# RMSNorm factors applied at other places of a one-core decoder step on Trainium2

## The chip, the cores and the metric

The kernel runs on one core of one Trainium2 chip. The metric is the device time of one execution in microseconds. A kernel's time is the median of several runs; the profile is of one execution of its own.

## The reference, cut to what matters

One step of a decoder trunk for 256 prompt tokens and 8 x 4 sample tokens, 288 in all, 2048 features, all f32:

```python
def rmsnorm(x, g):
    return x * rsqrt(mean(x * x, -1) + EPS) * g

x = x + mixing_block(rmsnorm(x, norm_mix))       # w_in, convolutions, gated scan, w_out
k, v = rmsnorm(mem, norm_mem) @ (w_k, w_v)       # 256 memory tokens
x = x + cross_attention(rmsnorm(x, norm_xattn), k, v)   # w_q, scores, values, w_o
x = x + hier_moe(rmsnorm(x, norm_moe))           # logits = h @ (wg, we) + bias, top-2 experts of 16
y = rmsnorm(x, norm_final)
```

RMSNorm multiplies each token by a factor of its own (1/rms) and each feature by a weight of its own (the gain). A product h @ w may take the token's factor before or after it; the gain belongs to the features that the product sums over, so it must stand before it.

## The kernel before, in words

Activations are kept transposed, features on the 128 partitions: xT, hT and mT (the memory) have 16 blocks of [128, 288] (256 for the memory). Each engine has a program of its own; they meet at semaphores.

**Projections** (`project`, L730 to L761). A weight matrix is cut into tiles of 512x512 (1 MB). w_in (first of three parts) has 16 tiles, w_mid 8, w_last 16, w_k 16, w_out 16, w_q 16, w_v 16, w_o 16. Each tile is multiplied by a seven-product scheme of Strassen's kind on 2x2 blocks. That needs sums of weight blocks, which GpSimd makes per tile in four operations (`sum_tile`, L652 to L657), and sums of activation blocks, which VectorE makes per group of four blocks in four operations (`h_sums`, L1414 to L1422). Four tiles (one column group) accumulate in PSUM; VectorE combines the seven products in place in six operations (`combine`, L1441 to L1447), and ScalarE copies the result out. PSUM has eight banks in two halves of four; units of work take the halves in turn (`start_unit` waits until the half is read out, `half_free`).

**Loads.** SyncE (SP) issues nearly all loads in program order: x, 16 small loads of norm weights, biases and states (`pack`), the memory, the gate weights, then the weight tiles into a ring whose places TensorE frees. GpSimd and TensorE wait for each tile.

**Entry.** TensorE transposes x (three chunks of tokens), the memory (two) and pack (L695). VectorE squares x; a matmul with a column of 1/2048 sums the squares (`stat`, L722), VectorE copies the partial sums, a second matmul with ones adds and spreads them (L727), ScalarE takes the root, VectorE the reciprocal (`apply_norm`, L1469) and multiplies each block by weight and factor (L1471), with `h_sums` after every fourth block. The first matmul of w_in needs the first group. The memory takes the same way.

**Mixing block.** After w_in come the gates (`gates(0)`, L778, 16 small matmuls), w_mid, gates again, w_last; GpSimd and VectorE do the scan. The key projection runs (`project_memory`, L799), its last four tiles behind `mix_stat`; VectorE normalises the 16 blocks of the mixed output in two halves (L1643), each fourth followed by `h_sums`, and after them combines the last key columns (`combine_memory("w_k", 3)`). ScalarE evicts these at L1234, TensorE transposes the states (L836), w_out starts.

**Cross-attention and router.** After w_out VectorE adds the result to xT (`add_residual`, L1650 to L1658), ScalarE squares it, statistic, root, reciprocal, normalisation with sums, w_q. After w_o the same, into hT; then the router's 16 matmuls, a copy, three small products that give the logits by token, three times 16 transposes of h for the experts (h_tok, evicted by ScalarE), and the choice of experts on VectorE (from L1754). The experts' weights stream through 12 slots.

## Time and profile before

| | us |
|---|---|
| runs | 1607.52, 1609.87, 1611.09 |
| median | 1609.87 |
| the profiled execution: its own time | 1609.71 |
| its span in the profile | 1608.0 |
| TensorE (matmul) busy | 1483.1 (92%) |
| GpSimd busy | 657.1 (41%) |
| VectorE busy | 583.6 (36%) |
| ScalarE busy | 175.2 (11%) |
| read from memory | 369.3 MB, 234 GB/s over the span |

Own time and span differ by 1.7 us around the profile's first and last instruction. On the chain of work that ended last, TensorE holds 85% of the span, VectorE 11%, ScalarE 2%. TensorE's two clock levels are 1.2 and 2.4 GHz; the profile gives the granted clock as a share of the higher one, 0.96 on the mean. "Idle before" names how long an engine stood before an operation and what released it.

### The profile page before, as it was taken

The page shows a single profiled execution, that of the slowest core. Times are in us where ns is not written, and L with a number is a line of the kernel's source. Part 1 is how long each engine was busy: PE and PEld are TensorE (multiplying, and loading weights), DVE is VectorE, ACT ScalarE, POOL GpSimd, SP SyncE. Part 2 cuts the span into 40 slices and gives each one's busy share as a digit, 9 for nine tenths or more (in the row PEclk, how much of TensorE's full clock was granted, in tenths as well). Part 3 has the DMA queues.
Part 4 walks back from the last instruction along what each step waited for, and adds up shares of the span by engine and source line. Part 5 has one row for each costly group of instructions (what it writes and reads, how often), then busy time and mean ns, then how long its engine had stood idle before and what let it go on. Part 6 is the DMA issues. An engine that isn't in the chain of part 4 may idle for free.

```text
span 1608.0 us, 24420 instructions
## 1 busy us (share of the span) xinstructions
PE 1483.1 (92%) x9906; PEld 1154.6 (72%) x9906; DVE 583.6 (36%) x1042; ACT 175.2 (11%) x281; POOL 657.1 (41%) x498
## 2 busy tenths in 40 slices
PE   5789999999959979999999899869999999999996
PEld 3789999998859969988777699754554454545534
DVE  3927668749561241112111621241212112212204
ACT  3000221000000000012222100121000000000002
POOL 4557697879947737753444557200000000000000
PEclk9889999999979989999999999979999999999998
DMA  7234444445534434463888434808999999999971
GB/s 236 79 118 145 130 158 131 157 157 186 174 104 147 153 105 150 146 259 128 325 327 330 146 132 157 340 1 354 397 422 399 396 423 397 379 423 397 400 311 59
DMA packets 106097, 376.99 MB, mean 234 GB/s; under 512 B 12405, under 2 KB 12405, under 8 KB 76274
## 3 DMA queue, kind: packets, MB, share of 16 engines
q1 hardware_dynamic: 103762, 371.68, 61.3%
q10 hardware_dynamic: 2272, 4.42, 0.8%
q8 instruction: 45, 0.74, 0.2%
q14 instruction: 18, 0.15, 0.0%
HBM read 369.30 MB, written 6.77 MB: 234 GB/s over the span
## 4 chain that ended last, share of the span: by engine, by line
PE 85%; DVE 11%; ACT 2%; issue 1%; DMA 1%; DVEq 0%; ACTq 0%; SPq 0%
PE ps L752 36%; PE ps L1048 14%; PE ps L799 11%; PE ps L1096 7%; PE ps L1110 4%; PE ps L1026 4%; PE ps L856 2%; DVE hT L1471 2%; DVE hT L1643 1%; PE ps L1065 1%; PE ps L874 1%; PE ps L864 1%; DVE hT L1420 1%; DMA A<-in_x_sample 1%; PE ps L695 1%
## 5 line engine op out<-in xcount | busy, mean ns | idle before, releaser
L752 PE MATMUL ps<-hT,tiles 128*128 128x144 f32 x2816 | 470.7, 291 | 49.3 <-ACT kv_stage L1234 16.8
L752 PEld LDWEIGHTS ps<-hT,tiles 128*128 128x128 f32 x2816 | 401.6, 194 | 52.8 <-issue 23.8
L652 POOL TENSOR_TENSOR tiles<-tiles 128x512 f32<-128x512 f32 x88 | 123.4, 1402 | 228.8 <-DMA tiles<-in_w_in 89.8
L1048 PE MATMUL ps<-tiles,A 128*64 128x512 f32 x576 | 171.2, 601 | 1.3 <-DVE A L1876 1.3
L752 PE MATMUL ps<-tiles 128*128 128x144 f32 x960 | 172.1, 289 | 0.0
L1441 DVE COPY pair_sums<-ps 128x144 f32<-128x144 f32 x44 | 13.5, 308 | 354.6 <-PE ps L752 354.6
L752 PEld LDWEIGHTS ps<-tiles 128*128 128x128 f32 x960 | 141.3, 193 | 0.0
L752 PE MATMUL ps<-A,tiles 128*128 128x144 f32 x768 | 138.2, 289 | 0.0
L799 PE MATMUL ps<-tiles,mT 128*128 128x256 f32 x512 | 133.3, 383 | 4.1 <-ACT kv_stage L1234 4.1
L655 POOL TENSOR_TENSOR tiles<-tiles 128x512 f32<-128x512 f32 x88 | 122.8, 1396 | 0.0
L657 POOL TENSOR_TENSOR tiles<-tiles 128x512 f32<-128x512 f32 x88 | 118.3, 1344 | 6.9
L654 POOL TENSOR_TENSOR tiles<-tiles 128x512 f32<-128x512 f32 x88 | 118.0, 1341 | 6.9
L1048 PEld LDWEIGHTS ps<-tiles,A 128*64 128x64 f32 x576 | 52.9, 138 | 88.3 <-issue 86.2
L752 PEld LDWEIGHTS ps<-A,tiles 128*128 128x128 f32 x768 | 113.5, 193 | 0.0
L1096 PE MATMUL ps<-tiles,mT 128*64 128x512 f32 x448 | 113.3, 597 | 0.0
L1048 PE MATMUL ps<-A 128*64 128x512 f32 x384 | 112.9, 593 | 0.0
L799 PEld LDWEIGHTS ps<-tiles,mT 128*128 128x128 f32 x512 | 94.0, 191 | 23.2 <-ACT kv_stage L1234 6.8
L799 PE MATMUL ps<-tiles,A 128*128 128x256 f32 x384 | 103.8, 379 | 0.0
L642 POOL TENSOR_TENSOR tiles<-tiles 128x512 f32<-128x512 f32 x32 | 45.6, 1425 | 101.5 <-DMA tiles<-in_xa_w_v 91.7
L1887 DVE TENSOR_TENSOR mT<-mT,ps 64x512 f32<-64x512 f32 x16 | 11.0, 689 | 201.9 <-ACT mT L1348 201.9
L799 PEld LDWEIGHTS ps<-tiles,A 128*128 128x128 f32 x384 | 73.0, 190 | 9.9
L1096 PEld LDWEIGHTS ps<-tiles,mT 128*64 128x64 f32 x448 | 36.7, 138 | 54.1 <-issue 54.1
(287 smaller groups left out, 1741.6 us busy)
## 6 DMA issues: line engine op xcount, KB each, us to landing
tiles<-in_expert_w_down SPq DMA_DIRECT2D x56, 1024.0 KB, 10.0
tiles<-in_w_in SPq DMA_DIRECT2D x40, 1024.0 KB, 5.1
tiles<-in_expert_w_gate SPq DMA_DIRECT2D x40, 1024.0 KB, 11.3
A<-in_expert_w_up SPq DMA_DIRECT2D x32, 1024.0 KB, 9.4
tiles<-in_expert_w_up SPq DMA_DIRECT2D x32, 1024.0 KB, 12.6
...
```

The costliest lines, as they stand in the source:

```text
L642: step.tick(tt(t1, b12, b11, ALU.subtract))
L652: step.tick(tt(s1, a21, a22, ALU.add))
L654: tt(a21, a11, a21, ALU.subtract)
L655: step.tick(tt(s2, s1, a11, ALU.subtract))
L657: tt(s4, a12, s2, ALU.subtract).then_inc(weights_summed, 1)
L752: return mm(one(u + mp, x, TH), w[:, kp, mp, :], rhs, start=(first and g == 0 and kp == 0), stop=(g == 3 and kp == 1), skip_group_check=True)
L799: return mm(one(u, x, TW // 2), own, w[:, kp, :], start=(first and g == 0 and kp == 0), stop=(g == 3 and kp == 1), skip_group_check=True)
L856: m = nc.tensor.transpose(attention_bank(i % 2)[:, b * P:(b + 1) * P], cache_tile(tile)[:, (4 * (i % 4) + b) * P:(4 * (i % 4) + b + 1) * P ...
L1026: mm(ps[:, b // 4, b % 4 * P:(b % 4 + 1) * P], h_tok[:, c, b * P:(b + 1) * P], pick[:, c, :], start=(b % 4 == 0 and c == 0), stop=False, s ...
L1048: m = mm(ps[C * n:C * n + C, BRANCH_BANK, :], xe[:, b, C * s:C * s + C], moe_tile(t + 2 * g + n).rearrange("p (k n) -> p k n", k=KT)[:, k, :],
L1096: m = mm(ps[C * s:C * s + C, 4 + b, :], actT[:, s, k, :], moe_tile(16 + 2 * k + s)[:, b * TW:(b + 1) * TW], start=(k == 0), stop=(k == KT ...
L1110: m = mm(ps[:, scatter_bank(q) + b, 0:T], y_pair[:, j * P:(j + 1) * P], spread[:, :], start=True, stop=True)
```

## The change

At five places the factors of RMSNorm are put elsewhere.

1. **Entry.** x's tokens lie on the partitions when they are loaded. ScalarE squares each chunk with a running sum, takes the root; VectorE takes the reciprocal and scales the identity by it (`diag`). The product of a chunk of x with this diagonal is the transposed chunk times its factors (`turn_scaled`); the weights are applied when it is evicted, half by VectorE, half by ScalarE (`scaled_out`). The statistics on TensorE go. x is still transposed as it is, too: chunk 0 before, chunks 1 and 2 after. The load of x has three semaphores; pack's loads go to ScalarE's queue; the first four tiles of w_in are issued right after x, memory and gate weights after them.
2. **Memory.** Its two diagonal products come between w_in and the gates.
3. **w_k.** `combine_memory("w_k", 3)` comes after blocks 0 to 7 of the mixed output instead of after all 16.
4. **w_out to w_q.** `add_residual` also multiplies by the weights alone and makes the sums; w_q runs on that. The statistic's matmuls come after w_q's fourth tile, the product with ones after its fifth, in a spare bank; the queries are multiplied by the factors at their eviction by VectorE (group 0 afterwards). Arrays change places in memory.
5. **Router.** hT gets the weights alone, too. Per group of four blocks come the router's matmuls, the statistic's, and between them the first transposes for the experts. The logits and the statistic are brought to the tokens together; ScalarE takes the root (`token_root`), VectorE multiplies the logits by the factor, ScalarE multiplies h_tok at its eviction.

The diff, cut to its core; the pieces are SyncE's loads, TensorE's program (entry, memory, w_q, router), ScalarE's (squares, eviction), and VectorE's (entry, mixed output, `add_residual`, queries, logits):

```diff
-sp.dma_start(x_nat[:, 0:2, :], a["x_prompt"][0].rearrange("(c p) d -> p c d", p=P)).then_inc(x_loaded, 16)
-sp.dma_start(x_nat[0:NB * ST, 2, :], a["x_sample"].rearrange("b t d -> (b t) d")).then_inc(x_loaded, 16)
...
+for c in range(2):
+    sp.dma_start(x_nat[:, c, :], a["x_prompt"][0, c * P:(c + 1) * P, :]).then_inc(x_loaded[c], 16)
+sp.dma_start(x_nat[0:NB * ST, 2, :], a["x_sample"].rearrange("b t d -> (b t) d")).then_inc(x_loaded[2], 16)
+def load_mem_and_gates():
+    sp.dma_start(mem_nat[:, :, :], a["mem_prompt"][0].rearrange("(c p) d -> p c d", p=P)).then_inc(mem_loaded, 16)
...
+if name == "w_in" and j == RAW - 1:
+    load_mem_and_gates()
...
+def turn_scaled(u, src, scale, rows):
+    start_unit(pe, u)
+    for b in range(DB):
+        m = mm(bank(u, b // 4)[:, b % 4 * P:b % 4 * P + rows], src[:, b * P:(b + 1) * P], scale,
+               start=True, stop=True)
+    m.then_inc(unit_done, 1)
+turn_x(UNIT["x"], 0)
 for c in range(3):
     rows = P if c < 2 else NB * ST
-    turn(UNIT["x"] + c, lambda b: x_nat[0:rows, c, b * P:(b + 1) * P], rows)
-pe.wait_ge(mem_loaded, 16)
+    pe.wait_ge(diag_ready, c + 1)
+    turn_scaled(UNIT["h"] + c, x_nat[0:rows, c, :], diag[0:rows, c, 0:rows], rows)
 for c in range(2):
-    turn(UNIT["mem"] + c, lambda b: mem_nat[:, c, b * P:(b + 1) * P], P)
-pe.wait_ge(pack_loaded, 16 * 16)
-turn(UNIT["pack"], lambda b: pack[0:NROWS, b * P:(b + 1) * P], NROWS, GB)
+    turn_x(UNIT["x_rest"] + c, c + 1)
...
-stat("x_stat", [(mean_d, hT, range(DB), T)], squares_ready, (1, 1, 0), groups=False)
-stat("mem_stat", [(mean_d, mem_sq, range(DB), NM)], mem_sq_ready, (2, 2, 1), groups=False)
...
+project("w_in", 2, hT, h_sums_in)
+pe.wait_ge(mem_loaded, 16)
+for c in range(2):
+    pe.wait_ge(mem_diag_ready, 1)
+    turn_scaled(UNIT["mem"] + c, mem_nat[:, c, :], diag[:, c, :], P)
 pe.wait_ge(wbd_loaded, 16 * 4)
 pe.wait_ge(xc_ready, 1)
 gates(0)
...
+project("w_out", 2, hT, h_sums_out)
+spare_bank = lambda mp: ps[:, 4 * ((UNIT["w_q"] + mp) % 2) + 3, 0:T]
+for j in range(16):
+    project_tile("w_q", j, h_res, h_sums_q)
+    if j == 3:
+        for k in range(DB):
+            if k % 4 == 0:
+                pe.wait_ge(squares_ready, 1 + k // 4 + 1)
+            c = 32 * (k % 4)
+            m = mm(spare_bank(0)[c:c + 32, :], mean_d[:, :], sq_res[:, k, :], start=(k < 4), stop=(k >= DB - 4))
+        m.then_inc(unit_done, 1)
+    if j == 4:
+        pe.wait_ge(partial_ready, 2)
+        mm(spare_bank(1), ones[:, :], rstd[:, 0, :], start=True, stop=True).then_inc(unit_done, 1)
...
+def route(g):
+    pe.wait_ge(h_ready, 4 * HREADY["moe"] + g + 1)
+    for k in range(4 * g, 4 * g + 4):
+        c = 32 * (k % 4)
+        mm(bank(u, 0)[c:c + 32, 0:T], wr[:, k, :], hT[:, k, :], start=(k < 4), stop=(k >= DB - 4))
+    pe.wait_ge(squares_ready, 5 + g + 1)
+    for k in range(4 * g, 4 * g + 4):
+        c = 32 * (k % 4)
+        m = mm(bank(u, 1)[c:c + 32, 0:T], mean_d[:, :], sq_res[:, k, :], start=(k < 4), stop=(k >= DB - 4))
+    return m
...
+for g in range(3):
+    route(g)
+start_unit(pe, UNIT["h_tok"])
+turn_tokens(0, range(12))
+route(3).then_inc(unit_done, 1)
+turn_tokens(0, range(12, 16)).then_inc(unit_done, 1)
+pe.wait_ge(logits_in, 1)
+pe.wait_ge(stat_out, 1)
 for c in range(3):
     own = rstd[:, 0, c * P:(c + 1) * P] if c < 2 else rstd[:, 1, 0:P]
-    m = mm(bank(u, c)[:, 0:NG + NE], own, same_logit[:, :], start=True, stop=True)
+    mm(bank(u, 2)[:, 32 * c:32 * c + NG + NE], own, same_logit[:, :], start=True, stop=True)
+    m = mm(bank(u, 2)[:, 32 * c + 20:32 * c + 21], stat_sum[:, c * P:(c + 1) * P], ones[:, 0:1], start=True, stop=True)
...
+    fn(spare[0:rows, :], x_nat[0:rows, c, :], ACT.Square, accum_out=mean_sq[0:rows, c:c + 1]).then_inc(squared, 1)
+    act.wait_ge(squared, c + 1)
+    fn(token_rstd[0:rows, c:c + 1], mean_sq[0:rows, c:c + 1], ACT.Sqrt, scale=1.0 / D,
+       bias=consts[0:rows, 0:1]).then_inc(mean_root, 1)
+def scaled_out(name, u, dst, rows):
+    for b in range(GB):
+        r = ROWS[name] + 1
+        m = fn(dst[:, GB + b, 0:rows], bank(u, 2 + b // 4)[:, b % 4 * P:b % 4 * P + rows], ACT.Copy,
+               scale=vec[:, b, r:r + 1])
+    m.then_inc(half_free[u % 2], 1)
...
+def make_diag(c):
+    rows = P if c < 2 else NB * ST
+    dve.wait_ge(mean_root, c + 1)
+    then(v.reciprocal(token_rstd[0:rows, c:c + 1], token_rstd[0:rows, c:c + 1]))
+    ts(diag[0:rows, c, 0:rows], ident[0:rows, 0:rows], token_rstd[0:rows, c:c + 1], None, ALU.mult
+       ).then_inc(diag_ready, 1)
+def scaled_out(name, u, dst, rows):
+    gains = vec[:, :, ROWS[name]].rearrange("p (b k) -> p b k", k=4).unsqueeze(3).broadcast_to([P, 2, 4, rows])
+    tt(dst[:, 0:GB, 0:rows].rearrange("p (b k) n -> p b k n", k=4), from_banks(u, rows)[:, 0:2], gains, ALU.mult
+       ).then_inc(half_free[u % 2], 1)
+make_diag(0)
+u = UNIT["x"]
+after_event(dve, EVENT["x"])
+v.tensor_copy(quads(xT[:, :, 0:P]), from_banks(u)).then_inc(half_free[u % 2], 2)
+make_diag(1)
+read_out(dve, UNIT["pack"])
 for c in range(3):
-    read_out(dve, UNIT["x"] + c)
-tt(hT[:, :, :], xT[:, :, :], xT[:, :, :], ALU.mult).then_inc(squares_ready, 1)
-read_out(dve, UNIT["pack"])
-lam = vec[:, :, ROWS["rg_lambda"]]
-stt(out=small[:, 0, :], in0=lam, scalar=-1.0, in1=lam, op0=ALU.mult, op1=ALU.max).then_inc(lam_in, 1)
+    after_event(dve, EVENT["h"] + c)
+    scaled_out("norm_mix", UNIT["h"] + c, hT[:, :, c * P:T], P if c < 2 else NB * ST)
+    if c == 0:
+        make_diag(2)
...
+for g in range(4):
+    h_sums(hT, h_sums_in, g)
+u = UNIT["x_rest"] + 1
+after_event(dve, EVENT["x_rest"] + 1)
+v.tensor_copy(quads(xT[:, :, 2 * P:T]), from_banks(u, NB * ST)).then_inc(half_free[u % 2], 2)
...
-            h_sums(h_sums_out, 2 * n + b // 4)
-combine_memory("w_k", 3)
-def add_residual(name):
+            h_sums(hT, h_sums_out, 2 * n + b // 4)
+    if n == 0:
+        combine_memory("w_k", 3)
...
+        for mp in range(2):
+            read_out(dve, group_unit(name, g, mp))
+        for b in range(4 * g, 4 * g + 4):
+            m = ts(dst[:, b, :], xT[:, b, :], gain(norm, b), None, ALU.mult)
+        if sums is not None:
+            then(m)
+            h_sums(dst, sums, g)
+        else:
+            m.then_inc(h_ready, 1)
+add_residual("w_out", "norm_xattn", h_res, h_sums_q)
...
+def evict_queries(g, scaled):
+    for mp in range(2):
+        u = group_unit("w_q", g, mp)
+        combine_pair("w_q", g, mp)
+        dve.wait_ge(combined, 2 * (GROUP["w_q"] + g) + mp + 1)
+        q = qT[:, 4 * g + 2 * mp:4 * g + 2 * mp + 2, :]
+        if scaled:
+            tt(q, half(u, T, 2), rstd[:, 0, :].unsqueeze(1).broadcast_to([P, 2, T]), ALU.mult
+               ).then_inc(half_free[u % 2], 2)
+        else:
+            v.tensor_copy(q, half(u, T, 2)).then_inc(half_free[u % 2], 2)
+evict_queries(0, False)
+after_event(dve, EVENT["xattn_stat"])
+v.tensor_copy(rstd[:, 0, :], ps[:, 4 * (UNIT["w_q"] % 2) + 3, 0:T]).then_inc(partial_ready, 1)
+dve.wait_ge(xattn_root, 1)
+then(v.reciprocal(rstd[:, 0, :], rstd[:, 0, :]))
+for mp in range(2):
+    read_out(dve, group_unit("w_q", 0, mp))
+tt(qT[:, 0:4, :], qT[:, 0:4, :], rstd[:, 0, :].unsqueeze(1).broadcast_to([P, 4, T]), ALU.mult
+   ).then_inc(first_queries_ready, 1)
+for g in range(1, 4):
+    evict_queries(g, True)
...
+dve.wait_ge(token_root, 1)
+then(v.reciprocal(h_rstd[:, 0:3], h_rstd[:, 0:3]))
 for c in range(3):
-    m = tt(lg[:, c, :], bank(u, c)[:, 0:NG + NE], rbias[:, :], ALU.add)
+    m = stt(out=lg[:, c, :], in0=bank(u, 2)[:, 32 * c:32 * c + NG + NE], scalar=h_rstd[:, c:c + 1], in1=rbias[:, :],
+            op0=ALU.mult, op1=ALU.add)
```

**TensorE at the entry**, before: transposes (L695: x in three rows, memory within the third, pack last), statistics, then w_in at the branch of its loop.

```order
L695 MATMUL ps<-ident,A 128x128 x32
L695 MATMUL ps<-ident,A 128x32 x16
L695 MATMUL ps<-ident,A 128x128 x32
L695 MATMUL ps<-ident,A 128x71 x8
L722 MATMUL ps<-hT,mean_d 32x288 x16
L727 MATMUL ps<-rstd,ones 128x288
L722 MATMUL ps<-A,mean_d 32x256 x16
L727 MATMUL ps<-rstd,ones 128x256
L736 UNCONDITIONAL_BRANCH
```

Now (L690 transposes, L708 products with the diagonal, `rstd` being where the diagonal lies):

```order
L690 MATMUL ps<-ident,A 128x71 x8
L690 MATMUL ps<-ident,A 128x128 x16
L708 MATMUL ps<-rstd,A 128x128 x32
L708 MATMUL ps<-rstd,A 128x32 x16
L690 MATMUL ps<-ident,A 128x128 x16
L690 MATMUL ps<-ident,A 128x32 x16
L778 UNCONDITIONAL_BRANCH
```

Pack is first; the memory and both statistics are gone from here; the branch is w_in's loop.

**VectorE at the end of the mixing block**, before: the third and fourth group of four normalised blocks (L1643) with their sums, then the combine of the last key columns (`tiles<-ps`).

```order
L1420 TENSOR_TENSOR hT<-hT 128x2x144
L1421 TENSOR_TENSOR A<-hT,A 128x288
L1422 TENSOR_TENSOR A<-hT,A 128x288
L1643 SCALAR_TENSOR_TENSOR hT<-hT,vec,rstd 128x288 x4
L1419 TENSOR_TENSOR A<-hT 128x288
L1420 TENSOR_TENSOR hT<-hT 128x2x144
L1421 TENSOR_TENSOR A<-hT,A 128x288
L1422 TENSOR_TENSOR A<-hT,A 128x288
L1441 COPY tiles<-ps 128x256
L1442 TENSOR_TENSOR tiles<-ps,tiles 128x256
L1443 TENSOR_TENSOR ps<-ps,tiles 128x256
L1445 TENSOR_TENSOR tiles<-ps,tiles 128x512
L1446 TENSOR_TENSOR ps<-ps,tiles 128x512
```

Now the same, from the second group on (L1745 is the old L1643, L1514 to L1517 the sums, L1536 to L1542 the combine):

```order
L1745 SCALAR_TENSOR_TENSOR hT<-hT,vec,rstd 128x288 x4
L1514 TENSOR_TENSOR A<-hT 128x288
L1515 TENSOR_TENSOR hT<-hT 128x2x144
L1516 TENSOR_TENSOR A<-hT,A 128x288
L1517 TENSOR_TENSOR A<-hT,A 128x288
L1536 COPY tiles<-ps 128x256
L1537 TENSOR_TENSOR tiles<-ps,tiles 128x256
L1538 TENSOR_TENSOR ps<-ps,tiles 128x256
L1540 TENSOR_TENSOR tiles<-ps,tiles 128x512
L1541 TENSOR_TENSOR ps<-ps,tiles 128x512
L1542 TENSOR_TENSOR ps<-ps,tiles 128x256
L1745 SCALAR_TENSOR_TENSOR hT<-hT,vec,rstd 128x288 x4
```

The combine stands behind the second group's sums instead of the fourth's; the third and fourth group follow it.

**TensorE between w_out and w_q**, before: the end of w_out's loop, the statistic (L722, L727), the loop of w_q.

```order
L736 COMPARE_AND_BRANCH
L722 MATMUL ps<-A,mean_d 32x288 x16
L727 MATMUL ps<-rstd,ones 128x288
L736 UNCONDITIONAL_BRANCH
L736 ISA
L313 ISA
L752 MATMUL ps<-hT,tiles 128x144 x2
```

Now (L756 is the old L752, L862 and L866 the statistic, L881 the values stage behind w_q):

```order
L778 COMPARE_AND_BRANCH
L756 MATMUL ps<-A,tiles 128x144 x112
L862 MATMUL ps<-A,mean_d 32x288 x16
L756 MATMUL ps<-A,tiles 128x144 x28
L866 MATMUL ps<-rstd,ones 128x288
L756 MATMUL ps<-A,tiles 128x144 x308
L881 MATMUL ps<-ident,tiles 128x128 x8
```

w_q begins at once (112 matmuls are its first four tiles), the statistic and the product with ones lie inside it.

## Rows read from the trace of the kernel before

**Rows 1.** Stretches by engine: stretch, us, busy PE, PEld, DVE, ACT, POOL, clock, DMA, GB/s
```profile
24.00:25.00 1.00, 1.00 (x11) 1.00 (x10) 1.00 (x1) 0.24 (x1) 0.88 (x1) 0.94 1.04 401
50.00:55.00 5.00, 5.00 (x24) 5.00 (x23) 4.83 (x12) 0.00 (x0) 0.00 (x0) 0.52 0.00 0
147.00:174.00 27.00, 27.00 (x218) 26.78 (x217) 19.93 (x34) 1.16 (x2) 20.11 (x16) 1.00 0.46 150
456.00:457.00 1.00, 0.00 (x0) 0.00 (x0) 1.00 (x1) 0.00 (x0) 0.76 (x1) 1.00 0.24 90
582.00:595.00 13.00, 3.60 (x34) 1.25 (x34) 8.58 (x18) 1.66 (x2) 5.05 (x4) 0.70 0.23 81
1087.00:1567.00 480.00, 477.62 (x2613) 233.32 (x2611) 86.99 (x144) 30.55 (x55) 0.00 (x0) 0.99 0.95 393
```
**Rows 2.** Timeline, TensorE at the entry: start us, us, engine, operation [idle before <-releaser]
```profile
11.57 7.57 PE L695 MATMUL ps<-ident,A 128*128 128x128 f32 x48 [11.57 <-DMA A<-in_x_sample]
21.43 4.99 PE L695 MATMUL ps<-ident,A 128*128 128x128 f32 x32 [2.29 <-ACT xT L1153]
48.95 1.32 PE L752 MATMUL ps<-hT,tiles 128*128 128x144 f32 x4 [10.55 <-DVE tiles L1422]
```
**Rows 3.** Timeline, TensorE at the fifth tile of w_in
```profile
87.02 1.33 PE L752 MATMUL ps<-hT,tiles 128*128 128x144 f32 x4 [7.50 <-ACT A L1185]
```
**Rows 4.** Timeline, ScalarE, GpSimd and VectorE at the entry
```profile
30.37 1.91 ACT L1159 ACTIVATE A<-mT 128x2048 f32<-128x2048 f32 x1
...
24.12 3.34 POOL L652 TENSOR_TENSOR tiles<-tiles 128x512 f32<-128x512 f32 x1 [19.96 <-DMA tiles<-in_w_in]
46.17 1.36 POOL L657 TENSOR_TENSOR tiles<-tiles 128x512 f32<-128x512 f32 x1
64.25 4.41 POOL L652 TENSOR_TENSOR tiles<-tiles 128x512 f32<-128x512 f32 x1 [16.72 <-DMA tiles<-in_w_in]
...
45.01 1.40 DVE L1419 TENSOR_TENSOR tiles<-hT 128x288 f32<-128x288 f32 x1
47.77 0.45 DVE L1421 TENSOR_TENSOR tiles<-hT,tiles 128x288 f32<-128x288 f32 x1
```
**Rows 5.** DMA issues: count, KB each, median us from issue to landing
```profile
A<-in_x_prompt SPq DMA_DIRECT2D x1, 2048.0 KB, 8.3
out_p_mem_k<-kv_stage ACTq DMA_DIRECT2D x4, 512.0 KB, 2.9
out_p_mem_v<-kv_stage ACTq DMA_DIRECT2D x4, 512.0 KB, 9.2
```
**Rows 6.** Timeline, TensorE at the first gates (L778) and in the experts (L1026)
```profile
175.96 2.37 PE L778 MATMUL ps<-A,kv_stage 128*128 128x312 f32 x8 [0.68 <-ACT A L1195]
179.12 0.73 PE L752 MATMUL ps<-hT,tiles 128*128 128x144 f32 x4 [0.79 <-ACT A L1203]
...
1116.88 2.94 PE L1026 MATMUL ps<-A 128*128 128x128 f32 x24
```
**Rows 7.** Timeline, key projection to w_out: TensorE, VectorE, ScalarE
```profile
451.51 1.04 PE L836 MATMUL ps<-ident,states 128*54 128x128 f32 x8
469.39 1.33 PE L752 MATMUL ps<-hT,tiles 128*128 128x144 f32 x4 [16.85 <-ACT kv_stage L1234]
...
448.06 1.41 DVE L1422 TENSOR_TENSOR A<-hT,A 128x288 f32<-128x288 f32 x1
465.38 0.42 DVE L1441 COPY tiles<-ps 128x256 f32<-128x256 f32 x1
468.33 1.01 ACT L1234 COPY kv_stage<-ps 128x1024 f32<-128x1024 f32 x1 [39.99 <-DVE ps L1447]
```
**Rows 8.** Timeline, TensorE at the start of w_q
```profile
595.25 1.32 PE L752 MATMUL ps<-hT,tiles 128*128 128x144 f32 x4 [6.51 <-DVE A L1422]
```
**Rows 9.** Timeline, VectorE: last residual addition behind w_o, first gate operation
```profile
1036.32 0.76 DVE L1658 TENSOR_TENSOR xT<-xT,ps 128x576 f32<-128x576 f32 x1
1056.37 0.17 DVE L1754 TENSOR_REDUCE mT<-mT 128x3 f32<-128x12 f32 x1
```

More of the change, by code:

```diff
@@ L227, in build @@
         place_gate, at = cut(at, 2)
+        h_rstd, at = cut(at, 4)
         silu, at = cut(at, TW)
@@ L772, in gates, with project @@
+            def project(name, pairs, h, sums):
+                with pe.Fori(0, pairs) as i:
+                    for j in range(8):
+                        project_tile(name, j, h, sums, i)
             def gates(h):
```

331 lines of the change are left out of this document (169 added, 162 removed).

## The prediction

> **What bounds the kernel now.** I read the stretches by engine first, then the engines' timelines round every place where TensorE stands. Inside a projection TensorE is never idle: 218 matmul records fill 27.00 us, 0.124 us each, and a weight tile is 56 records, so 6.9 us [rows 1]. Inside the experts it is busy 477.62 of 480 us [rows 1]. So time can only be won between the stages, and whatever TensorE starts earlier there, everything behind it ends earlier. Five places matter.
>
> At the entry the first projection matmul starts at 48.95 us, after 10.55 us of waiting for VectorE's sums [rows 2]. It then runs at the lower clock (granted 0.52 over 50 to 55, the 1.2 GHz level; 24 records in 5 us) [rows 1]; I put the end of tile 0 at 58.8 (24 records by 54.8, 32 more at 0.124). Four tiles later TensorE stands again until 87.02, 7.5 us, since VectorE first works off some forty small preparatory operations, many of them beside a working GpSimd [rows 3]; it comes back at the lower clock (four records in 1.33 us), about 5.9 us at half speed, 2.9 us lost. Between the key projection and w_out it waits 16.85 us for an eviction that ScalarE makes at 468.33, once VectorE has combined the last key columns, which stands behind all 16 normalised blocks [rows 7]. Between w_out and w_q it does 3.60 us of work in 13 us [rows 1] and starts w_q at 595.25 at the lower clock [rows 8]. Behind w_o the last residual addition ends at 1037.08, and the first gate operation starts only at 1056.37 [rows 9].
>
> **The change, part by part.** The sum is made against the profiled execution's own 1609.71 us (span 1608.0); the median of the runs, 1609.87, is practically the same.
>
> Entry. Removed ahead of the projection: three transposes of x in a row, the memory's transposes and squares, both statistics, the root with its table load, a reciprocal, 16 normalisations. Added: pack and x0 transposed, then products of x with a diagonal. The w_in loads are issued right behind x, the pack's 16 small loads on ScalarE's queue.
> - x_prompt's 2 MB landed 8.3 us after issue [rows 5]; its first half now has its own semaphore. ScalarE issues 16 loads (0.3 us each, to 5.7), loads a table, squares each chunk in about 1.9 us [rows 4]: the first two roots are there by 12, before TensorE wants them.
> - The pack is first in TensorE's order. When it lands is not shown; a load on ScalarE's queue beside few others took 2.9 us, beside a full SP queue 9.2 [rows 5]. From the last issue at 5.4 that is 8.3 or 14.6. These are a few rows, not 512 KB, so I take 9.5.
> - Pack and x0 transposes: 48 transposes took 7.57 us at the start [rows 2], so about 3.5 us for 24: 13.0. A chunk's product is 16 matmuls, 32 records, at 0.12 (24 in 2.94 us [rows 6]) or twice that at the lower clock. With the rise some 6 us after TensorE's first work: 17.8, 21.3, and 22.9 for the sample rows.
> - ScalarE evicts half a chunk by 8 small activations (2.0 us; last 24.8), so VectorE begins its 16 sum operations at 24.9. Beside a working GpSimd each takes 1.40 us, alone 0.45 [rows 4]. GpSimd starts when w_in tile 0 lands, about 13 (2.36 MB of x, then 1 MB, at some 400 GB/s), and its 16 operations, 24.12 to 47.5 before [rows 4], now last to about 34.5. So: 7 slow ones, 9 quick ones, 39.0. Only then VectorE copies out the sample rows of x, which free the half for the second half of tile 0: **late next** is this copy, 39.8. Tile 0 ends at about 44.0. Gain 58.8 - 44.0 = **14.8**. Bounds: all 16 quick and no late pack, 36; all slow with the pack at 14.6, 56.
> - VectorE's preparatory work then falls into GpSimd's pause (waiting for tile 4, as in the 16.72 us before [rows 4]) and ends near 48; its first combine is due at 61. The stall and its cold restart go: **10.4** (0 if that work took 13 us more).
>
> The memory products, 32 matmuls or 64 records, come between w_in and the gates: 64 x 0.12 = 7.7, of which the 0.8 us that TensorE waited there covers a little. Their evictions, the table load and four sigmoids follow; second gate product and the next projection started at 175.96 and 179.12 [rows 6]; I count 184.9. Cost **5.8** (4.5 to 8). The eviction of group 3 and the gates queue behind it by the same amount.
>
> Key projection to w_out. The combine moves ahead of blocks 8 to 15. TensorE ends the projection at 451.5, VectorE the second sums at 449.47 [rows 7]; combine (2.9, its time before, 465.4 to 468.3), eviction 1.0: w_out starts at 455.9 instead of 469.39, **13.5**. The third and fourth sums are done by 476 even if all their operations are slow, when tiles 2 and 3 want them at 469.6 and 476.5: just covered; late next are these. An idle stretch from 452.5 had not lowered the clock by 457 [rows 1], so half of the 2.6 us of restart, **1.3**, may go too (0 to 2.6).
>
> w_out to w_q. Squares, statistic, root, reciprocal and normalisation leave the gap; 16 products with a weight vector and 16 sum operations move beside w_out, where VectorE mostly waits for TensorE. The statistic's 32 records and the ones product stay on TensorE, 2.7 us, inside w_q. The queries' evictions move from ScalarE to VectorE, hidden by tiles of 6.9 us. Gap 13.3 (582 to 595.25) - 2.7 + 2.9 of slow restart = **13.5** (11 to 15).
>
> Behind w_o. Of 1037.1: four products with the weights 1.3, last route 1.6, transposes beside it, copy 0.8, 12 short matmuls 1.6, ScalarE's copy of h and table load (1043 to 1044.2), root 0.2, reciprocal and logits 0.6: gate operations at 1045.1 instead of 1056.37 [rows 9], **11.1**. Everything behind keeps its order, the scaled token copies cost no more than the copies. Bounds 8 and 13. The experts' first 12 tiles wait for w_o's tiles, not for the router, and are there either way.
>
> Sum: 14.8 + 10.4 - 5.8 + 13.5 + 1.3 + 13.5 + 11.1 = 58.8; 1609.71 - 58.8 = 1550.9, so **1551 us**.
>
> **A rule against the trace.** At 24 to 25 us the granted clock is already at 0.94 [rows 1], while TensorE had done nothing but transposes since 21.43 [rows 2]: here they did raise it. The Trainium skill (TensorE: Matmul & The Clock Gate, Part 4: PE-mode transpose) states that transposes do not count as work for this. By that rule the first diagonal products would start the count: all 32 records of the first chunk slow, 2 us more, a sum of 1553.
>
> **The rivals.**
> - The entry gains less: the pack's small loads come through only behind SP's queue (9.2 against 2.9 us [rows 5]), or VectorE's sums all run beside GpSimd. For it: 16 loads against 6 MB in flight. Against: they are few packets. With the pack at 14.6 everything ahead of tile 0 moves by 5, and contention may add 5: 1556 to 1561.
> - Transposes do not raise the clock: 1553. Against it speaks the rise at 24; for it, that the 48 transposes before showed no quicker pace in 6 us. The page named above states it.
> - w_out starts early but waits: the sums of blocks 8 to 15 come late at tile 2 or 3, since VectorE has them behind the combine. For it: only 0.8 us of cover at tile 3. It gives back up to 7 us: 1558.
> - The change does not free the logits or w_q: a wait on a root takes the place of the statistic's (the router's root behind ScalarE's copy and table load, say). One of the two gains gone: 1562 to 1565.
> - Slower: GpSimd becomes the bound. Its four sums per tile take about 5.4 us (1.36 each beside VectorE [rows 4]), against TensorE's 6.9. The weight products and sums now run on VectorE beside w_out and w_o, and each locks with a GpSimd operation. From 6.9 us per tile this decides; to eat the 58.8 us over the 32 tiles of w_out and w_o a tile would have to take 8.7 us, its four operations 2.2 each; the one of 3.34 us [rows 4] shows that such operations exist, beside a very long one of VectorE. At 9 us per tile, 32 x 2.1 = 67 us against the gain: 1618.
>
> **How the numbers follow.** Forecast as worked out 0.58; smaller entry gain 0.17; transposes not counted 0.08; w_out waits 0.07; one gap kept 0.07; slower 0.03. A measurement of this kernel tells about 0.2% (3 us) from no change; all cases but the last are far beyond it, so faster 0.96, same 0.01, slower 0.03. The likeliest case, with its unknown costs, spans 1544 to 1557; the range takes in the smaller entry gain and most of the kept gap: 1542 to 1565.
>
> **What would show it.** Right: first projection matmul near 31 us, its second half near 40, no stall at tile 4; the next stage's first matmul 5.8 us later after w_in than before; w_out 4.4 us behind the key projection; w_q with no pause; gate operations 8 us behind the last residual addition. The pack's landing shows in TensorE's first start. Wrong would make it: a pause inside w_out, VectorE's sums beginning after 30, or a new wait for a root.

## The result and the profile after

The changed kernel takes **1560.91 us** (median of 4 runs, 1556.5 to 1562.6) against 1608.83 for the kernel before (4 runs, 1607.52 to 1611.09): a ratio of 0.9698, 95% interval 0.9674 to 0.9723. That is faster, inside the range, and 9.9 us above the forecast of 1551. The profiled execution took 1561.65 (span 1559.9).

The page's first part of the kernel after (busy time, share of the span, instructions):

```profile
span 1559.9 us, 24563 instructions
...
PE 1482.5 (95%) x9970; PEld 1162.9 (75%) x9970; DVE 560.4 (36%) x1028; ACT 182.8 (12%) x323; POOL 651.3 (42%) x498
```

TensorE has as much to do as before; 48 us of standing are gone. Where, its timeline tells (start us, us, operation, idle before and releaser; a row's xN counts matmul records, of which an f32 product has two and a transpose one), first at the entry, against [rows 2]:

```profile
15.67 4.59 PE L690 MATMUL ps<-ident,A 71*128 71x71 f32 x24 [15.67 <-DMA A<-in_norm_final]
20.05 11.58 PE L708 MATMUL ps<-rstd,A 128*128 128x128 f32 x96
31.56 5.52 PE L690 MATMUL ps<-ident,A 128*128 128x128 f32 x32
38.39 1.32 PE L756 MATMUL ps<-hT,tiles 128*128 128x144 f32 x4 [1.32 <-DVE tiles L1517]
```

The first projection matmul comes at 38.39 instead of 48.95. But pack, whose last row (norm_final) is waited for, landed at 15.67; I had put it at 9.5. Then, from the memory products to w_q, against [rows 6, 7, 8]:

```profile
152.18 7.31 PE L708 MATMUL ps<-rstd,A 128*128 128x128 f32 x64
159.32 2.27 PE L788 MATMUL ps<-A,kv_stage 128*128 128x312 f32 x8
161.75 2.37 PE L788 MATMUL ps<-A,kv_stage 128*128 128x312 f32 x8 [0.17 <-ACT mT L1219]
164.91 0.73 PE L756 MATMUL ps<-hT,tiles 128*128 128x144 f32 x4 [0.79 <-ACT A L1272]
...
441.52 0.76 PE L756 MATMUL ps<-hT,tiles 128*128 128x144 f32 x4 [3.18 <-ACT kv_stage L1306]
447.34 0.76 PE L756 MATMUL ps<-hT,tiles 128*128 128x144 f32 x4 [2.12 <-ACT kv_stage L1322]
...
581.30 2.15 PE L862 MATMUL ps<-A,mean_d 128*32 128x288 f32 x32
590.35 0.65 PE L866 MATMUL ps<-rstd,ones 128*128 128x288 f32 x2
```

w_out starts 3.2 us behind the key projection. The wait of 2.12 us at 447.34 is new: ScalarE's copy of the states, which frees TensorE's next half of PSUM, stands behind the store of the last key columns. No pause stands between w_out and w_q; the statistic (2.15) and the ones product (0.65) lie inside w_q. And the router, VectorE and TensorE, against [rows 9]:

```profile
996.44 0.75 DVE L1762 TENSOR_TENSOR xT<-xT,ps 128x576 f32<-128x576 f32 x1
1004.75 0.17 DVE L1890 TENSOR_REDUCE mT<-mT 128x3 f32<-128x12 f32 x1
```

```profile
1004.77 3.68 PE L1023 MATMUL ps<-ident,hT 128*128 128x128 f32 x16 [2.46 <-DVE mT L1904]
1011.18 3.67 PE L1023 MATMUL ps<-ident,A 128*128 128x128 f32 x16 [2.73 <-ACT A L1400]
1026.61 9.39 PE L1065 MATMUL ps<-A 128*128 128x128 f32 x64 [7.77 <-DVE A L1998]
```

The kernel before took 1.97 us for the third row of transposes, not 3.67, and had its experts' first products 18.35 us behind the first gate operation (1056.37), not 21.86:

```profile
1062.70 1.97 PE L1004 MATMUL ps<-ident,A 128*128 128x128 f32 x16 [1.98 <-ACT A L1325]
1074.72 1.65 PE L1026 MATMUL ps<-A 128*128 128x128 f32 x6 [7.77 <-DVE A L1866]
```

The stretches of the kernel after show why (columns as in [rows 1]):

```profile
30.00:31.00 1.00, 1.00 (x10) 1.00 (x10) 0.00 (x0) 0.00 (x0) 0.93 (x1) 0.85 0.35 54
31.00:38.00 7.00, 6.07 (x35) 5.54 (x35) 5.02 (x5) 4.21 (x10) 6.67 (x5) 0.50 0.03 6
441.52:445.40 3.88, 3.69 (x28) 3.48 (x28) 3.81 (x5) 0.00 (x0) 3.07 (x3) 1.00 0.51 186
886.08:892.98 6.90, 6.90 (x42) 6.90 (x43) 1.73 (x4) 0.00 (x0) 0.00 (x0) 0.75 0.07 7
1003.00:1026.00 23.00, 11.33 (x50) 10.72 (x50) 11.55 (x74) 9.07 (x11) 0.00 (x0) 0.51 0.00 1
```

The granted clock is 0.51 over the router's transposes and places (the short matmuls behind them that give each token its place in an expert); 0.75 in w_o's second half tile and the next, where 42 records fit into 6.9 us (in the kernel before it was 1.00 at that place, 56 records); it fell within 30 to 31, ahead of w_in; but it is 1.00 at w_out's start, where the kernel before had it low (0.56 over its first 6 us).

### The profile page after: what moved, and what is told of

Same layout as the page of the kernel before. It is cut to its first block, busy times and chain, and to the rows that moved or that the text cites. A ratio compares the mean times of both kernels' runs of the same rounds, so it can differ in the third digit from the quotient of the medians.

```text
span 1559.9 us, 24563 instructions
## 1 busy us (share of the span) xinstructions
PE 1482.5 (95%) x9970; PEld 1162.9 (75%) x9970; DVE 560.4 (36%) x1028; ACT 182.8 (12%) x323; POOL 651.3 (42%) x498
## 4 chain that ended last, share of the span: by engine, by line
PE 91%; DVE 5%; ACT 2%; DMA 1%; issue 1%; ACTq 0%; DVEq 0%
PE ps L756 38%; PE ps L1087 14%; PE ps L813 13%; PE ps L1135 7%; PE ps L1149 4%; PE ps L1065 4%; PE ps L881 2%; PE ps L708 1%; PE ps L1104 1%; PE ps L899 1%; PE ps L889 1%; PE ps L947 1%; DMA A<-in_norm_final 1%; PE ps L1073 1%; PE ps L920 0%
## 5 line engine op out<-in xcount | busy, mean ns | idle before, releaser
L756 PE MATMUL ps<-hT,tiles 128*128 128x144 f32 x1792 | 295.5, 288 | 8.9 <-ACT kv_stage L1306 3.2
L756 PE MATMUL ps<-A,tiles 128*128 128x144 f32 x1792 | 264.1, 288 | 7.3 <-DVE mT L1517 4.0
L756 PEld LDWEIGHTS ps<-hT,tiles 128*128 128x128 f32 x1792 | 251.6, 191 | 10.7 <-issue 3.7
L756 PEld LDWEIGHTS ps<-A,tiles 128*128 128x128 f32 x1792 | 239.1, 191 | 8.5 <-issue 4.9
L647 POOL TENSOR_TENSOR tiles<-tiles 128x512 f32<-128x512 f32 x88 | 117.4, 1334 | 194.3 <-DMA tiles<-in_w_in 83.8
L756 PE MATMUL ps<-tiles 128*128 128x144 f32 x960 | 171.1, 287 | 0.0
L756 PEld LDWEIGHTS ps<-tiles 128*128 128x128 f32 x960 | 140.3, 191 | 0.0
L1536 DVE COPY pair_sums<-ps 128x144 f32<-128x144 f32 x44 | 13.5, 308 | 322.3 <-PE ps L756 322.3
L650 POOL TENSOR_TENSOR tiles<-tiles 128x512 f32<-128x512 f32 x88 | 122.1, 1388 | 0.0
L652 POOL TENSOR_TENSOR tiles<-tiles 128x512 f32<-128x512 f32 x88 | 119.2, 1354 | 6.9
L649 POOL TENSOR_TENSOR tiles<-tiles 128x512 f32<-128x512 f32 x88 | 117.7, 1337 | 6.9
L637 POOL TENSOR_TENSOR tiles<-tiles 128x512 f32<-128x512 f32 x32 | 45.6, 1424 | 102.2 <-DMA tiles<-in_xa_w_v 92.0
## 6 DMA issues: line engine op xcount, KB each, us to landing
tiles<-in_expert_w_gate SPq DMA_DIRECT2D x40, 1024.0 KB, 11.3
```

The costliest lines, as they stand in the source:

```text
L637: step.tick(tt(t1, b12, b11, ALU.subtract))
L647: step.tick(tt(s1, a21, a22, ALU.add))
L649: tt(a21, a11, a21, ALU.subtract)
L650: step.tick(tt(s2, s1, a11, ALU.subtract))
L652: tt(s4, a12, s2, ALU.subtract).then_inc(weights_summed, 1)
L756: return mm(one(u + mp, x, TH), w[:, kp, mp, :], rhs, start=(first and g == 0 and kp == 0), stop=(g == 3 and kp == 1), skip_group_check=True)
```

## The account

Each row is the difference of the same event in the two profiled executions, less that of the rows above; the sum is the difference of the spans, and the rows add up to it within their rounding. A restart is what TensorE loses at the lower clock behind a pause.

| place | forecast | measured | from |
|---|---|---|---|
| tile 0 of w_in | 14.8 | 10.6 | 48.95 to 38.39, both with a slow start |
| stall at tile 4, restart | 10.4 | 10.3 | 173.02 to 152.18, less the 10.6 |
| memory products | -5.8 | -6.6 | 179.12 to 164.91 leaves 14.2 |
| w_out's start | 13.5 | 13.7 | 469.39 to 441.52 |
| w_out's restart, new wait, w_q | 1.3 + 13.5 | 13.6 | values stage 710.84 to 669.35 |
| attention and w_o | 0 | -1.6 | last addition 1036.32 to 996.44 |
| router | 11.1 | 11.7 | 1056.37 to 1004.75 |
| gates to experts | 0 | -3.5 | 1074.72 to 1026.61 |
| sum | 58.8 | 48.1 | spans 1608.0 to 1559.9 |

## The experiments

(The expectations put the fall of the clock at the entry at 30.85 and in the router at 1003.75; from the granted shares, 0.85 over 30 to 31 and 0.75 over 1003 to 1004, it is 30.7 and 1003.5.)

All but the first change the changed kernel. Noise first: runs of one kernel spread by some 6 us (1556.5 to 1562.6 for the changed one), so differences of 2 to 3 us between two variants are read from the places in the trace, not from the medians. A trace is one execution, and where the clock falls in it varies too.

**One part alone.** The kernel before, with only the combine moved:

```diff
                         h_sums(h_sums_out, 2 * n + b // 4)
-            combine_memory("w_k", 3)
+                if n == 0:
+                    combine_memory("w_k", 3)
```

> The kernel before with one part of the change alone: the combine of the last key columns after blocks 0 to 7 of the mixed output instead of after all 16. Theory (the parts add up): w_out starts 13.6 us earlier, its slow restart (2.9 us) goes since the clock has not fallen by then, and 2.1 us come back in w_out's first tile, because ScalarE's copy of the states waits there for the store of the last key columns. Together -14.4: 1594.5 us. Rival (the gain in the changed kernel comes from TensorE, VectorE and the loads standing otherwise there; alone, the sums of blocks 8 to 15 come late at tile 2 or 3): a wait of several us inside w_out, 1598 to 1602.

Measured 1592.26 (ratio 0.9899, 0.9876 to 0.9922), 15.9 us under the kernel before, 1608.17 beside it. TensorE's timeline of this kernel:

```profile
452.69 0.76 PE L752 MATMUL ps<-hT,tiles 128*128 128x144 f32 x4 [3.18 <-ACT kv_stage L1234]
456.57 0.76 PE L752 MATMUL ps<-hT,tiles 128*128 128x144 f32 x4 [0.18 <-ACT kv_stage L1250]
```

The sums of blocks 8 to 15 are never late. The wait behind the states is only 0.18 us here; it follows the store of the last key columns, which took 4.7 us in the changed kernel's execution. That term of the theory, 2.1, was not there; without it the theory gives 16.5, and 15.9 were measured. So this part stands by itself.

**The states in columns of their own**, so that ScalarE does not wait for that store:

```diff
-        states_nat = kv_stage[:, :, :, :].rearrange("p a b c -> p (a b c)")[:, 0:RG]
+        states_nat, _ = cut(9216, RG)
...
-            act.wait_ge(kv_stored[0], 16 * 2)
-            act.wait_ge(kv_stored[1], 16 * 2)
```

> The changed kernel with the states evicted into columns of their own instead of into the key columns' staging buffer, so that ScalarE's copy of them no longer waits for the stores of the key columns. Theory: the wait of 2.12 us in w_out's first tile (447.34) goes, 2.1 us less: 1558.8. Rival: something else holds that tile's second half (the weights' sums on GpSimd or the activations' sums on VectorE), and under 0.5 us of it goes: 1560.5 or more.

1558.88 (0.9675, 0.9651 to 0.9699). The wait is gone from the trace, so nothing else holds that half. The 2.0 us of the medians agree, but lie within the noise. In the profiled execution, the slowest of the four, the clock had fallen by w_out's start (four records in 1.33 us instead of 0.76), which took the gain back:

```profile
441.89 1.33 PE L756 MATMUL ps<-hT,tiles 128*128 128x144 f32 x4 [3.19 <-ACT kv_stage L1306]
```

**w_q's part taken back**: statistic, root and normalisation between the projections again, queries evicted by ScalarE.

```diff
+            stat("xattn_stat", [(mean_d, sq_res, range(DB), T)], squares_ready, (1, 2, 0))
+            project("w_q", 2, h_res, h_sums_q)
...
+            for b in range(DB):
+                m = stt(out=h_res[:, b, :], in0=xT[:, b, :], scalar=gain("norm_xattn", b), in1=rstd[:, 0, :],
```

> The changed kernel with the part between w_out and w_q taken back: residual additions without the weights, the statistic, root, reciprocal, normalisation and sums between the two projections, and the queries evicted by ScalarE. Theory (the parts add up; this one gave 12.6 us in the trace): w_q starts about 13.3 us behind w_out's end, at the lower clock; 1573.5 us. Rival (beside w_out the weight products and sums hold GpSimd, whose operations lock with VectorE's, so that part of the gain is given back there): taking it back costs less, 1570 or under, and w_out's sixteen tiles take less time than the 110.6 us (16 tiles of 6.9) of the changed kernel.

1572.49 (0.9758, 0.9735 to 0.9781), 11.6 above the changed kernel. In the trace the stretch from w_out's start to the values stage is 682.19 - 441.22 = 241.0 against 227.8: 13.1 us, the forecast's term being 13.5. Beside w_out a record takes as long in both, 0.123 us (865 in 106.0 us, 797 in 97.7): nothing is given back there, and GpSimd as the bound falls. The two executions differ at w_out's start, but not in time: here the clock was low from 442.7 to 446.1, and the wait for the states was 0.45 instead of 2.12 (first row below), so that the second half tile starts 5.8 us behind w_out's start in both.

```profile
447.03 0.76 PE L756 MATMUL ps<-hT,tiles 128*128 128x144 f32 x4 [0.45 <-ACT kv_stage L1310]
...
566.58 33.70 PE L756 MATMUL ps<-A,tiles 128*128 128x144 f32 x250 [6.51 <-DVE A L1506]
...
682.19 1.97 PE L870 MATMUL ps<-ident,tiles 128*128 128x128 f32 x8 [2.78 <-ACT hT L1252]
```

**The entry: TensorE's order turned.** x and its first diagonal product ahead of pack.

```diff
-            turn(UNIT["pack"], lambda b: pack[0:NROWS, b * P:(b + 1) * P], NROWS, GB)
             turn_x(UNIT["x"], 0)
...
                 turn_scaled(hu(UNIT, c), x_nat[0:rows, c, :], diag[0:rows, c, 0:rows], rows)
+                if c == 0:
+                    pe.wait_ge(pack_loaded, 16 * 16)
+                    turn(UNIT["pack"], lambda b: pack[0:NROWS, b * P:(b + 1) * P], NROWS, GB)
```

> The changed kernel with TensorE's order at the entry turned: chunk 0 of x and its product with the diagonal first, then pack, then chunks 1 and 2; and VectorE copies the sample rows of x after the first group's sums instead of after all four. Theory (pack's landing at 15.67 us is what the entry lost): TensorE starts at about 9 instead of 15.67, the last diagonal product ends at about 25 instead of 31.6, the first matmul of w_in comes at 32 to 33 instead of 38.39, limited by GpSimd, which now runs beside all of the first sums. 5 to 6 us less than the changed kernel: 1555 to 1556. Rival (VectorE's sums beside GpSimd set the start, not pack): the first matmul comes later than 35.5 and the gain is under 3 us: 1558 or more. Rival on the clock: if it falls again while TensorE works on transposes and diagonal products, w_in's first 24 records are slow as before (no difference to the sum).

1558.45 (0.9686, 0.9665 to 0.9706). The first projection matmul moved by 2.4 us, not by 5 to 6: a miss.

```profile
5.97 3.34 PE L693 MATMUL ps<-ident,A 128*128 128x128 f32 x16 [5.97 <-DMA A<-in_x_prompt]
10.92 3.84 PE L709 MATMUL ps<-rstd,A 128*128 128x128 f32 x32 [1.61 <-DVE rstd L1481]
15.77 0.72 PE L693 MATMUL ps<-ident,A 71*128 71x71 f32 x8 [1.01 <-DMA A<-in_norm_final]
19.70 8.84 PE L709 MATMUL ps<-rstd,A 128*128 128x128 f32 x64 [3.21 <-DVE rstd L1481]
35.95 1.32 PE L760 MATMUL ps<-hT,tiles 128*128 128x144 f32 x4 [2.76 <-DVE tiles L1520]
...
17.38 2.18 ACT L1223 ACTIVATE hT<-ps,vec 128x128 f32<-128x128 f32 x8 [2.05 <-DVE vec L1497]
```

Pack's transposes still start at 15.77, the evictions need its weights, and chunk 1 needs the half that they free: ScalarE's ends at 19.56, and TensorE stands until 19.70. (The row names VectorE's diagonal, which ends at about the same time, but that is chunk 2's.)

**The weights of norm_mix ahead of pack**, with a semaphore of their own:

```diff
-                act.dma_start(pack[ROWS[name]:ROWS[name] + rows, :], src).then_inc(pack_loaded, 16)
+                act.dma_start(pack[ROWS[name]:ROWS[name] + rows, :], src
+                              ).then_inc(gain_loaded if name == "norm_mix" else pack_loaded, 16)
...
             turn_x(UNIT["x"], 0)
+            pe.wait_ge(gain_loaded, 16)
+            turn(UNIT["gain"], lambda b: pack[0:2, b * P:(b + 1) * P], 2, GB)
```

> The changed kernel with pack cut in two: the two rows of norm_mix are loaded first with a semaphore of their own and transposed right behind chunk 0 of x; the other rows are transposed behind x, ahead of w_in, and copied out after the first group's sums, as are the sample rows of x. So neither TensorE's first work nor the evictions of the diagonal products wait for pack. Theory (pack's late landing holds the evictions; that is why turning TensorE's order alone gave only 2.4 us at the first projection matmul): h chunk 0 done by 17, the last one by 22, VectorE's first sums from 24 to 30 beside GpSimd, first matmul of w_in at 30 to 32 instead of 38.39, 6.5 to 8.5 us less than the changed kernel: 1552 to 1554. Rival (the three halves of evicting, the alternation of the two halves of PSUM and a falling clock hold the chain, not pack): first matmul at 34 or later, 4 us or less.

1556.65 (0.9663, 0.9644 to 0.9683), between theory and rival: 4.5 us at the first matmul.

```profile
6.08 4.59 PE L691 MATMUL ps<-ident,A 128*128 128x128 f32 x24 [6.08 <-DMA A<-in_x_prompt]
13.49 13.25 PE L707 MATMUL ps<-rstd,A 128*128 128x128 f32 x96 [2.82 <-DVE xT L1497]
33.89 1.33 PE L759 MATMUL ps<-hT,tiles 128*128 128x144 f32 x4 [2.46 <-DVE xT L1581]
```

Pack is out of the chain; next stand VectorE's copy of x (2.82), the 96 records of the products (13.25 us, since up to 18 they ran at half the pace, instead of 11.58), and VectorE's first sums beside GpSimd, at 1.41 to 1.52 us each for three of four, and the copy of the sample rows behind them (L1581), for which TensorE waits last.

**Why pack was late.** w_in's loads only behind pack:

```diff
+            sp.wait_ge(pack_loaded, 16 * 16)
             load_matrix("w_in", w_in, 5, [None] * RAW + [(tile_used, n + 1) for n in range(RAW)])
```

> The changed kernel with w_in's loads issued only once pack has landed, so that pack's 16 small loads share the memory with x alone. Question: why pack landed at 15.67 us when its last load was issued at 6.33. Theory (the 4 MB of w_in, issued from 2.27 us, are in flight beside them): without them the last load lands 3 to 5 us after its issue, and TensorE starts at 10 to 12. Rival (a small load takes 9 us from issue to landing at this place in any case): TensorE starts at 15 to 16 as before. The total says little, since w_in's tiles now land later: 1555 to 1563.

```profile
6.05 0.30 ACTq L1204 DMA_DIRECT2D A<-in_norm_final  x1
...
13.90 4.15 PE L691 MATMUL ps<-ident,A 71*128 71x71 f32 x24 [13.90 <-DMA A<-in_norm_final]
```

One run, 1562.31. Even beside x alone the last small load took 7.8 us from its issue; w_in's traffic adds only 1.5 (9.3 before). So both theories missed, and the rival is nearer. The 2.9 us of [rows 5], from which I had taken 9.5, is no measure of 16 small loads issued behind one another; it is not even a load, but the median of four stores of 512 KB. Why the small loads take so long stays open.

**Why the clock fell at 30.7 us**, while TensorE had worked without a pause since 15.67. First, dense data in place of the diagonal:

```diff
-                turn_scaled(UNIT["h"] + c, x_nat[0:rows, c, :], diag[0:rows, c, 0:rows], rows)
+                turn_scaled(UNIT["h"] + c, x_nat[0:rows, c, :], x_nat[0:rows, c, 0:rows], rows)
```

> The changed kernel with the first projection's activations wrong: the three products at the entry take 128 columns of x itself as moving operand in place of the diagonal, same shapes and same waits. Values behind it, the router's choice too, differ, so only the trace up to 150 us is read. Question: why the granted clock fell at 30.85 us, when TensorE had worked without a pause since 15.67. Theory 1 (a product with a diagonal, nearly all zeros, holds the clock less than a dense one): granted 1.00 from 31 to 38, the 32 transposes behind take 3.7 instead of 5.52 us, and w_in starts at the higher clock. Theory 2 (the content doesn't matter): the fall stays within 2 us of 30.85 and w_in's first 24 records take 5.8 us as before.

The results behind it are not the model's, so only the entry is read (the time, 1623.07, says nothing). The clock fell just the same (0.71 over 30 to 31, 0.50 behind), the transposes took 5.51:

```profile
20.30 11.69 PE L708 MATMUL ps<-A 128*128 128x128 f32 x96
31.92 5.51 PE L690 MATMUL ps<-ident,A 128*128 128x128 f32 x32
```

The zeros are not the reason. Then the short product of the sample rows in the middle, by the order of the three:

```diff
-            for c in range(3):
+            for n, c in enumerate((0, 2, 1)):
```

> The changed kernel with the product of the sample rows (32 rows by 32 columns) between those of the two prompt chunks instead of behind them, all else equal. Question as in the run with dense products: why the granted clock fell at 30.85 us while TensorE worked. Theory 1 (the 16 small products, 3.5 us of short matmuls ahead of the fall, let it fall): no fall at 30 to 32, or one near 27, right behind the small products. Theory 2 (the fall comes some time after TensorE's start whatever it works on): 30 to 31 again. The time stays within 2 us of the changed kernel in either case.

One run, 1564.69 (3.8 above the changed kernel's median, over the 2 I had allowed, in one run). Its timeline and the stretch of the fall:

```profile
24.75 10.73 PE L708 MATMUL ps<-rstd,A 32*128 32x32 f32 x64 [0.73 <-DVE rstd L1482]
```

```profile
27.00:28.00 1.00, 1.00 (x8) 1.00 (x7) 0.00 (x0) 0.00 (x0) 1.00 (x2) 0.61 1.20 159
```

The short matmuls, which had begun at 27.5, now began at 24.75, and the fall moved from 30.7 to 27.2: it came 2.5 to 3.2 us behind their start, with the engine shown busy. In the six executions with the entry of the changed kernel (the dense one among them) it came at 29.6 to 31.3, so 27.2 is outside their spread, which speaks against theory 2; but it is one run, and it also has a pause of 0.73 us ahead of the short matmuls. Theory 1 is not shown either. With the norm_mix edit the same short matmuls ran from 23.0 to 26.7, and the clock stayed at 1.00 behind them until TensorE stood (it fell at 31.7):

```profile
26.00:27.00 1.00, 1.00 (x10) 0.96 (x10) 0.23 (x1) 0.23 (x2) 0.95 (x1) 1.00 0.98 383
27.00:28.00 1.00, 1.00 (x11) 1.00 (x10) 0.20 (x1) 1.00 (x8) 1.00 (x2) 1.00 1.21 217
```

It was the same in the run with w_in's loads behind pack (short matmuls from 25.7 to 29.4, fall at 34.5) and in the one with three edits; with TensorE's order turned the clock fell 0.8 us behind their end. So the short matmuls are not enough to let it fall. What else has to come together stays open.

**The router: idle TensorE filled.**

```diff
+            for k in range(5):
+                mm(bank(UNIT["router"], 3)[:, 0:T], ones[:, :], hT[:, k, :], start=True, stop=True)
...
+            start_unit(pe, UNIT["h_tok"] + 4)
+            for k in range(13):
+                mm(bank(UNIT["h_tok"] + 2, 3)[:, 0:T], ones[:, :], hT[:, k, :], start=True, stop=True)
```

> The changed kernel with idle TensorE filled in the router's section: 5 matmuls of 128x288 into an unused bank behind the logits and 13 behind the places, their results unused. Theory (3.5 us of the router's gain are lost since the granted clock falls at 1003.75 while TensorE stands, and the 32 transposes and the places' matmuls then run at the lower level): with the clock held, the places end 3.5 us earlier, and the experts' first 64 records take 7.7 instead of 9.39 us: together 3.5 to 5.2 us less than the changed kernel, 1556 to 1557.5. Rival (the chain there is ScalarE's copies and VectorE's choice, TensorE's pace is hidden): under 1 us, 1560 or more. The filler itself costs nothing if it ends ahead of what it stands before.

1560.23 (0.9688, 0.9668 to 0.9709): a miss.

```profile
1003.22 1.97 PE L1023 MATMUL ps<-ident,hT 128*128 128x128 f32 x16
1009.63 3.67 PE L1023 MATMUL ps<-ident,A 128*128 128x128 f32 x16 [4.45 <-ACT A L1405]
1025.55 7.31 PE L1070 MATMUL ps<-A 128*128 128x128 f32 x64
```

The first filler held the clock for the second row of transposes, 1.97 us, but the third row waits for ScalarE's eviction anyway, now for 4.45 instead of 2.73, and the clock fell there (it was low from 1007.5). The second filler brought it back for the experts' first 64 records, 7.31 instead of 9.39. Of 3.5 to 5.2 us some 1.6 came in the trace (last residual addition to the first expert tile), none that the runs can tell.

**The router: ScalarE's order.** The eviction that this row waits for, put between the two exponentials:

```diff
             fn(G(4), G(3), ACT.Exp).then_inc(gate_exp, 1)
+            act.wait_ge(token_rstd_ready, 1)
+            tokens_out(0)
             act.wait_ge(gate_in, 2)
             fn(G(17, 1), G(16, 1), ACT.Exp).then_inc(gate_exp, 1)
+            tokens_out(1)
+            tokens_out(2)
```

> The changed kernel with ScalarE's order in the router's section turned: the eviction of the first h_tok chunk between the two exponentials of the gates instead of behind both (it is ready at 1003.9, ScalarE stands from 1006.2 to 1009.07). Theory (the third row of transposes waits for this eviction, 2.73 us, and what it gains is not hidden by VectorE's choice, which is done at 1011.6): the third row starts 3 us earlier, the places and the experts' first products come 2.8 us earlier, 1558 us. Rival (TensorE's lower clock or VectorE's mask sets the places, so that the earlier start changes the place of the wait only): under 1 us.

1557.12 (0.9677, 0.9652 to 0.9701), 3.8 under the changed kernel.

```profile
1008.32 2.86 PE L1023 MATMUL ps<-ident,A 128*128 128x128 f32 x16
1011.51 0.40 PE L1055 MATMUL ps<-mT,A 128*128 128x16 f32 x2 [0.32 <-ACT A L1397]
1021.91 9.98 PE L1065 MATMUL ps<-A 128*128 128x128 f32 x64 [7.76 <-DVE A L2002]
```

The wait of 2.73 is gone, TensorE works on through both rows, the clock comes back within the second, and the experts' first products start 4.7 us earlier, the first expert tile 4.1 (1034.34 against 1038.46), with the last residual addition at the same time (996.51 against 996.44): more than the 3.5 us that this section had lost. The stretch in which the clock came back:

```profile
1010.00:1011.00 1.00, 1.00 (x10) 0.95 (x8) 0.83 (x6) 1.00 (x1) 0.00 (x0) 0.87 0.02 8
```

**Three edits together**: norm_mix first, states apart, ScalarE's order.

> Three of the edits together: the weights of norm_mix loaded and transposed ahead of pack, the states in columns of their own, and ScalarE's order in the router. Theory (independent places, their gains add): 4.5 + 2.1 + 2.8 = 9.4 us less than the changed kernel, 1551.5 us, ratio to the kernel before about 0.9645. Rival (the clock's restarts take part of it back, as one more idle stretch falls on a fall of the clock): 1553 to 1556.

**1552.64** (5 runs, 1550.23 to 1556.16; 0.9658, 0.9637 to 0.968). 8.3 us under the changed kernel, 1 short of the sum: within what a measurement tells. It beats both kernels, though its interval touches that of the changed one (0.9674).

## Why the prediction was right, and where it was off

- **The mechanism was right.** Time was won between the stages, and what was started earlier there moved all that is behind it. The range did not hold by errors that cancel: nearly all go one way, 4.2 us at the entry, 3.5 behind the gates and 1.6 in w_o of the 10.7 in all, and the range had 14 us of room above the forecast.
- **Entry, 14.8 forecast, 10.6 measured.** The step that failed is "These are a few rows, not 512 KB, so I take 9.5". Pack landed at 15.67, above even the late case of 14.6; this was the first rival, at 0.17, and it came true. (The 2.9 and 9.2 us that bound this term are called loads there; the rows show stores of 512 KB.) A second term was too small: 1.6 us for the product of the sample rows, whose 32 records took 4.1 us, 27.5 to 31.6, the last of it at the lower clock, and 3.75 in the run with the norm_mix edit, at the higher one. That is 0.117 us each, as much as a record of a full chunk. And GpSimd started at 16.78, not 13, as w_in's first tile landed later. As everything came later, GpSimd was done (at 37.8) when VectorE had made its first four sums, three of them slow and the next quick, so that the copy of the sample rows was no wait:

```profile
33.85 1.41 DVE L1515 TENSOR_TENSOR hT<-hT 128x288 f32<-128x288 f32 x1
...
38.07 0.45 DVE L1514 TENSOR_TENSOR tiles<-hT 128x288 f32<-128x288 f32 x1
```

- **The stall at tile 4** went as forecast, 10.3 against 10.4.
- **Memory, -5.8 forecast, -6.6 measured**: 7.14 us of products and 0.17 of wait; inside the bounds.
- **Combine, 13.5 forecast, 13.7 measured.** Late next were not the sums, as I had written (VectorE had the fourth group's at 452.6, 11 us behind w_out's start), but the copy of the states behind the store of the key columns: 2.1 us. (The cover of 0.8 us at tile 3 should read 0.5, 476.5 less 476.) For the restart I had put 1.3, half of 2.6. In this execution the clock stayed at 1.00 and all 2.6 went, which with the new wait leaves 0.5 (13.6 of that row, less 13.1 for w_q). That it stayed is luck: of the twelve profiled executions with the combine moved, in five it fell within 1.5 us of w_out's start (states apart, w_q taken back, TensorE's order turned, small product in the middle, filler).
- **w_out to w_q, 13.5 forecast, 13.1 in the run that takes it back.** The rival that GpSimd becomes the bound is refuted there, as w_out's records take 0.123 us in both.
- **Router, 11.1 forecast, 11.7 measured at the first gate operation.** (1056.37 less 1045.1 is 11.3, not the 11.1 of the sum.) The step that failed is "Everything behind keeps its order, the scaled token copies cost no more than the copies", which puts the rest at nothing: the copies did not cost more, but the clock did. Before, the router's own matmuls and the transposes behind them had brought it back by 1059; now it fell at 1003.5 and was low through the transposes, the places and half of the experts' first products: 3.5 us. Another 1.6 us went the same way in w_o (0.75 over 886 to 893, 14 records fewer in 6.9 us).
- **The rule on transposes.** The kernel before showed 0.94 over 24 to 25 with nothing but transposes since 21.43. The run with ScalarE's order agrees: behind the fall at the router TensorE did transposes alone from 1004.85 on, the clock rose within 1010 to 1011, and the third row took 2.86 us against 3.67. But they do not always bring it back: in the changed kernel TensorE did nothing but transposes from 31.6 to 37.1, the last 16 of 32 rows only, and the clock stayed at 0.50; with the states apart it rose at 34.6 in the same row. The Trainium skill (TensorE: Matmul & The Clock Gate, Part 4: PE-mode transpose) says that they do not count. For f32 transposes the measurements here decide against that as a general rule; when they do raise the clock stays open.
